# Order of the first transfers, casts and subtractions at the start of the first and of the merging run of a two-block kernel

## What is computed

```python
h = rms_norm(x, norm_w)
proj = h @ w_in
a_u, a_v, a_z, b_q, b_k, b_v, b_z, m_q, m_z, g = jnp.split(proj, split_at, axis=-1)
u = jax.nn.gelu(a_u, approximate=False)
vv = layer_norm(jax.nn.gelu(a_v, approximate=False), a_v_norm_w, a_v_norm_b)
y_a = chunked_spatial_gating(u, vv, a_spatial_w, a_spatial_b) * jax.nn.silu(a_z)
...
gates = jax.nn.sigmoid(g.reshape(bn, s, N_BRANCHES, D_MODEL) + gate_b)
merged = (gates[:, :, 0] * (y_a @ proj_a)
          + gates[:, :, 1] * (y_b @ proj_b)
          + gates[:, :, 2] * (y_m @ proj_m))
x = x + merged @ w_out
```

## Time and profile before

| | |
|---|---|
| median of 3 runs | 1872.83 us (1871.79 to 1872.91) |
| the profiled execution | 1871.02 us, its span 1869.2 us |
| TensorE busy | 1769.4 us |
| VectorE busy | 915.2 us |
| ScalarE busy | 654.0 us |
| GpSimd busy | 246.5 us |
| bytes moved | 123.07 MB, 66 GB/s over the span |

### The profile page before, as it was taken

How to read it: one execution, slowest core, us unless ns; L and a number is a source line. 1 busy time by engine, 2 the same in 40 slices (tenths; PEclk the granted TensorE clock), 3 DMA queues, 4 the chain that set the end, 5 groups by cost and what they waited for, 6 DMA issues and landing times. The chain is left out here.

```text
span 1869.2 us, 22280 instructions
## 1 busy us (share of the span) xinstructions
PE 1769.4 (95%) x8828; PEld 1435.2 (77%) x8828; DVE 915.2 (49%) x1504; ACT 654.0 (35%) x1204; POOL 246.5 (13%) x412
## 2 busy tenths in 40 slices
PE   6999989899999899799999999899999999999698
PEld 5788867688887788578888788688887777777587
DVE  5118887545334654383223322367142445657654
ACT  5224337512233333472212211233213353434531
POOL 3001210288601100000000000481000000000000
PEclk9999999899999999899999999899999999999799
DMA  4121100236322210111111121242623111000042
GB/s 137 51 68 46 46 22 3 87 104 185 109 80 88 75 34 23 59 43 43 51 51 54 40 58 30 79 150 79 140 50 93 34 35 35 23 23 35 23 147 102
DMA packets 146577, 123.07 MB, mean 66 GB/s; under 512 B 8859, under 2 KB 132106, under 8 KB 145802
## 3 DMA queue, kind: packets, MB, share of 16 engines
q1 hardware_dynamic: 146474, 121.65, 21.5%
HBM read 108.37 MB, written 13.26 MB: 65 GB/s over the span
## 5 line engine op out<-in xcount | busy, mean ns | idle before, releaser
L81 PE MATMUL psum<-hT,w_parts 128*128 128x512 f32 x3360 | 802.6, 396 | 20.1 <-DVE w_parts L182 13.4
L81 PEld LDWEIGHTS psum<-hT,w_parts 128*128 128x128 f32 x3360 | 634.5, 190 | 159.5 <-DVE w_parts L182 15.6
L182 DVE TENSOR_TENSOR w_parts<-w_raw,w_parts 128x1024 fp32r<-128x1024 f32 x104 | 133.1, 1280 | 491.4 <-ACT w_parts L178 491.2
L81 PE MATMUL psum<-h2T,w_parts 128*128 128x512 f32 x1248 | 300.6, 397 | 1.6 <-PEq L2144 1.1
L81 PEld LDWEIGHTS psum<-h2T,w_parts 128*128 128x128 f32 x1248 | 233.4, 190 | 51.3 <-issue 2.9
L81 PE MATMUL psum<-y_high,wp_parts 128*128 128x512 f32 x384 | 129.7, 398 | 9.6 <-DVE wp_parts L1421 9.3
L1373 ACT ACTIVATE gate<-psum,cols 128x512 f32<-128x512 f32 x48 | 33.1, 689 | 297.9 <-PE psum L81 297.9
L178 ACT CAST w_parts<-w_raw 128x1024 fp32r<-128x1024 f32 x104 | 108.3, 1041 | 74.6 <-DMA w_raw<-w_in 58.1
L81 PE MATMUL psum<-w_parts,y_parts 128*128 128x512 f32 x384 | 89.0, 394 | 7.7 <-DVE y_parts L1708 7.7
L81 PEld LDWEIGHTS psum<-y_high,wp_parts 128*128 128x128 f32 x384 | 72.5, 189 | 28.2 <-DVE wp_parts L1421 9.7
L81 PEld LDWEIGHTS psum<-w_parts,y_parts 128*128 128x128 f32 x384 | 73.2, 191 | 23.5 <-issue 8.1
(11 more groups left out here) (358 smaller groups left out, 2235.6 us busy)
## 6 DMA issues: line engine op xcount, KB each, us to landing
w_raw<-w_in SPq DMA_DIRECT2D x94, 512.0 KB, 3.9
middle_a<-ada_w SPq DMA_DIRECT2D x32, 384.0 KB, 3.6
w_raw<-w_out SPq DMA_DIRECT2D x16, 512.0 KB, 4.0
qkT<-x SPq DMA_DIRECT2D x8, 512.0 KB, 8.4
w_raw<-m_w_kv SPq DMA_DIRECT2D x8, 512.0 KB, 3.8
base<-x SPq DMA_DIRECT2D x8, 512.0 KB, 4.4
x_kept<-x_ring SPq DMA_DIRECT2D x8, 512.0 KB, 2.6
base<-x_kept SPq DMA_DIRECT2D x8, 512.0 KB, 3.6
```

Of the source, the lines that this page charges most:

```text
L81: last = pe.matmul(out, lhs(a, k), rhs(b, k), start=(k == 0 and n == 0), stop=(k == depth - 1 and n == 2))
L182: dve.tensor_tensor(self.parts[:, u, LO, :, :], self.raw[:, :, :], self.parts[:, u, HI, :, :].bitcast(F32), ALU.subtract).then_inc(self.lo ...
```

## The change

The first run: rows 2 and 3 of x are loaded ahead of the weights' first tile; ScalarE makes the roots of all four rows ahead of any cast; VectorE scales rows 2 and 3 ahead of moving rows 1 to 3 and of the weights' subtraction; TensorE turns four rows ahead of slot 0, and rows 4 and 5 within it. The merging run: the first tile of proj_b is the first load on the queue, the gate's second tile the second, and the three spatial loads come behind it (a new hook, `sync_second`); the two rows of y_b and the tile of proj_b are cast and subtracted ahead of everything else in `scalar_start` and `vector_start`.

```diff
@@ Dense.sync
                 w.load_tile(sp, self.tiles[n].view)
-            if n == 0:
-                for work in self.beside:
+            for work in self.beside:
+                if n == 0:
                     work.sync(sp, -1)
+                elif n == 1:
+                    work.sync_second(sp)
@@ FirstNorm
-        sp.dma_start(self.x[:, 1, :], self.src[1]).then_inc(self.x_loaded[1], 16)
+        for t in range(1, 4):
+            sp.dma_start(self.x[:, t, :], self.src[t]).then_inc(self.x_loaded[t], 16)
 
     def sync(self, sp, s):
         if s == -1:
-            for t in range(2, TT):
+            for t in range(4, TT):
                 sp.dma_start(self.x[:, t, :], self.src[t]).then_inc(self.x_loaded[t], 16)
...
         self.root(act, 2)
+        self.root(act, 3)
         self.split(act, 0)
+        self.split(act, 1)
         self.w.split_high(act, 0, 0)
-        self.root(act, 3)
-        self.split(act, 1)
-        self.root(act, 4)
         self.split(act, 2)
         self.split(act, 3)
+        self.root(act, 4)
         self.root(act, 5)
         self.w.split_high(act, 0, 1)
...
-        for t in range(TT):
-            self.scale(dve, t)
-            if t == 1:
-                dve.wait_ge(self.const_loaded, 32)
-            if t >= 1:
-                self.move(dve, t - 1)
-            if t == 2:
-                self.w.split_low(dve, 0, 0)
-            if t == 4:
-                self.split_low(dve, 3)
-            if t == 6:
-                self.w.split_low(dve, 0, 1)
+        self.scale(dve, 0)
+        self.scale(dve, 1)
+        dve.wait_ge(self.const_loaded, 32)
+        self.move(dve, 0)
+        self.scale(dve, 2)
+        self.scale(dve, 3)
+        for t in range(1, 4):
+            self.move(dve, t)
+        self.w.split_low(dve, 0, 0)
+        self.split_low(dve, 3)
+        self.scale(dve, 4)
+        self.scale(dve, 5)
+        self.move(dve, 4)
+        self.scale(dve, 6)
+        self.w.split_low(dve, 0, 1)
+        self.move(dve, 5)
+        self.scale(dve, 7)
+        self.move(dve, 6)
         self.move(dve, TT - 1)
...
-        for t in range(5):
+        for t in range(4):
             self.turn(pe, t)
...
-        if s in (0, 1):
-            self.turn(pe, 5 + 2 * s)
+        for t in {0: (4, 5), 1: (7,)}.get(s, ()):
+            self.turn(pe, t)
@@ Projections
+    def sync_start(self, sp):
+        self.load(sp, 0)
+
     def sync(self, sp, s):
-        if s == -1:
-            self.load(sp, 0)
-        elif s == 0:
+        if s == 0:
             self.load(sp, 1)
...
+    def scalar_start(self, act):
+        for r in self.splits(-1):
+            self.y_split_high(act, r)
+        self.wp_split_high(act, 0)
+
+    def vector_start(self, dve):
+        for r in self.splits(-1):
+            self.y_split_low(dve, r)
+        self.wp_split_low(dve, 0)
...
             self.y_split_high(act, r)
-        if s == 0:
-            self.wp_split_high(act, 0)
...
             self.y_split_low(dve, r)
-        if s == 0:
-            self.wp_split_low(dve, 0)
@@ SpatialValues
-    def sync(self, sp, s):
-        if s == -1:
-            sp.dma_start(self.wide, self.rows).then_inc(self.loaded, 16)
-            sp.dma_start(self.wT, self.spatial_dram).then_inc(self.loaded, 16)
-            sp.dma_start(self.bias, self.bias_dram).then_inc(self.loaded, 16)
+    def sync_second(self, sp):
+        sp.dma_start(self.wide, self.rows).then_inc(self.loaded, 16)
+        sp.dma_start(self.wT, self.spatial_dram).then_inc(self.loaded, 16)
+        sp.dma_start(self.bias, self.bias_dram).then_inc(self.loaded, 16)
@@ merge_run
-    split_at = {(1, 0): 0, (1, 1): 0, (2, 0): 12, (2, 1): 13, (2, 2): 14, (2, 3): 15, (0, 0): 28, (0, 1): 29}
+    split_at = {(1, 0): -1, (1, 1): -1, (2, 0): 12, (2, 1): 13, (2, 2): 14, (2, 3): 15, (0, 0): 28, (0, 1): 29}
```

More of the change, by code:

```diff
@@ L96, in sync_start @@
     def sync_start(self, sp):
+        pass
+    def sync_second(self, sp):
         pass
@@ L1432, in y_split_low @@
                           ALU.subtract).then_inc(self.y_low, 1)
+    def sync_start(self, sp):
+        self.load(sp, 0)
     def sync(self, sp, s):
-        if s == -1:
-            self.load(sp, 0)
-        elif s == 0:
+        if s == 0:
             self.load(sp, 1)
-        elif s % 2 and s // 2 + 2 < len(self.tiles):
+        elif s > 0 and s % 2 and s // 2 + 2 < len(self.tiles):
             self.load(sp, s // 2 + 2)
```

## The result

| | before | after |
|---|---|---|
| median, measured together | 1872.87 us (4 runs, 1871.79 to 1875.78) | 1858.74 us (4 runs, 1856.40 to 1859.85) |
| ratio | | 0.9916 [0.9901, 0.9931] |
| the profiled execution, its span | 1871.02, 1869.2 us | 1859.85, 1858.1 us |
| the same two kernels compared once more | 1873.30 us (11 runs) | 1859.65 us (6 runs), ratio 0.9929 [0.9914, 0.9943] |

The medians differ by 14.1 us in the first comparison and by 13.7 in the second; the ratios put it at 15.7 and 13.3. Between the two profiled executions the spans differ by 11.1.

What follows compares the result with a forecast made beforehand. TensorE, busy 1769.4 of 1869.2 us, was taken as the bound, with gains only where it waits or runs below full clock. -11.9 (merging run) - 0.8 (start) = -12.7, from 1872.83 to 1860.1 us; range 1857.2 to 1864.2.

Steps and rivals of the forecast that it cites:

- The forecast case: Whole kernel: merging run gains 11.9 us and the start 0.8, median 1860.1 us; chance 0.52.
- the start's term: First run: tile 0's second half starts at 41.1 instead of 41.88, 0.8 us gained of the first product's 2.5.
- The merging run's 11.9 us: Merging run: wait removed, 9.5 us, plus the clock no longer low behind it, 2.4 us.
- The wait removed, 9.5 us: Merging run, slot 0: TensorE no longer waits for the split of proj_b's first tile; 779.01 - 769.5 = 9.5 us.
- The clock behind it, 2.4 us: Merging run: with no pause the next 30 products take 6.87 us instead of 9.24, 2.4 us gained.
- rival 2: Merging run, slot 2: gate tile lands late, proj_b's second tile comes 2.2 us after TensorE; 1862.3 us, chance 0.10.
- The first product, 2.5 us earlier: Start: three operations of GpSimd and VectorE that exclude each other set the first product at 22.6 instead of 25.14.
- rival 1: Start: GpSimd served first at 34.6, row 7's scaling late, the start loses 1.5 us; 1862.4 us, chance 0.25.
- The start's two terms given back, 0.8 and 0.8: Start: row 4's transposes move into slot 0, +0.8 us; the longer standstill lowers the clock, 2.5 us lost against 1.7, +0.8.
- GpSimd's second group: Start: GpSimd works on row 4 from 32.2, ends row 6 about 39.9, holding row 7's subtraction until then, ending 41.0.
- Rival 3: Between the runs: the clock doesn't fall in the pause, 1.7 us more gained; 1858.4 us, chance 0.08.
- Rivals 4 and 5: Merging run's splits still late, 1872.0 us, chance 0.03; start slower through GpSimd winning five contested grants, 1875.4 us, chance 0.02.

Runs made afterwards that it cites:

- e2: Only the start's part of the change, the merging run as before, against the kernel before: 1871.18 us, ratio 1.0004 [0.9993, 1.0015].
- e8: The changed kernel with the gate's second tile loaded behind the three spatial loads: 1861.20 us, ratio to the kernel before 0.9931 [0.9916, 0.9946].
- e5: The changed kernel with row 2's low part on VectorE instead of GpSimd: 1859.25 us, ratio to the kernel before 0.9932 [0.9916, 0.9947].
- e1: Only the merging run's part of the change, the first run as before, against the kernel before: 1858.95 us, ratio 0.9937 [0.9923, 0.9950].
- the repeat: The changed kernel once more, unaltered, against the kernel before: 1859.65 us, ratio 0.9929 [0.9914, 0.9943].
- e3: The kernel before with only the merging run's new order of loads, casts and subtractions at their old places: 1868.18 us, ratio 0.9984 [0.9972, 0.9996].
- e11: The changed kernel with useless transposes in TensorE's pauses at the start and before the merging run: 1855.71 us, ratio to the kernel before 0.9898 [0.9883, 0.9913].
- e7: The changed kernel with 12 useless transposes at the end of the run before the merging run: 1859.29 us, ratio to the kernel before 0.9926 [0.9912, 0.9939].
- e10: The changed kernel with both of TensorE's pauses filled by useless transposes and row 2's low part on VectorE: 1854.03 us, ratio to the kernel before 0.9888.
- batch 1: The first group of follow-up runs on one chip, with the kernel before run beside them: 1871.89 us (21 runs, 1865.27 to 1876.12).
- e6: The changed kernel with 28 useless transposes while TensorE waits ahead of its first product: 1855.25 us, ratio to the kernel before 0.9911 [0.9894, 0.9927].
- e9: The changed kernel with the first run's loads in the old order, engines in the new: 1860.80 us, ratio to the kernel before 0.9926 [0.9913, 0.9940].

## Why the prediction was right in its mechanism, and where its size was wrong

The forecast case came in its mechanism, and more was gained than said: 14.1 us by the medians and 15.7 by the ratio, against 12.7. The median of 1858.74 us lies in the range, 1.4 us below the number. But by the ratio the time on the prediction's scale is 0.9916 x 1872.83 = 1857.1 us (1854.3 to 1859.9): 3.0 below the number and 0.1 below the range's lower end of 1857.2. The second comparison gives 1859.5 (1856.7 to 1862.1), inside the range. The gain of 12.7 us would be a ratio of 0.9932, just outside the first comparison's interval and inside the second's.

**The step that failed is the start's term, 0.8 us gained where the profile of after shows 2.2;** within it, above all, the 0.8 us given back to the clock, which was 0 there. The merging run's 11.9 us held (11.8). The second step is the range, which put the shifting of low clock in the untouched stretches at nothing. The bullets on the start, on what it is worth and on the span take these up.

- **The wait removed, 9.5 us.** Right. The projection of slot 0 moved by 9.42 us against the run's start. Its links held within 1 us: proj_b's cast at 764.06, the tile's subtraction ending at 765.5 (said: 766.4).
- **The clock behind it, 2.4 us.** Right: 30 products 6.88 us instead of 9.24. e2 shows the other side, where the wait came back and the 30 products behind it took 9.50 us again (781.41 to 790.91).
- **The gate tile and rival 2.** The tile landed early enough and the rival did not come about. Its condition and its place were right (e8: a wait of 2.43 us in slot 2, 2.2 said), but its price was too low by more than half. It counted the wait and not the clock that falls behind it; both together are 5.8 us in e8's profile.
- **The first product, 2.5 us earlier.** Right: 2.88 in the profile, 2.8 as mean. The three excluding operations are there one behind another, and e5, which moves one of them from GpSimd to VectorE, brings the product 1.2 us forward, as their sum gives. The Trainium skill, "SBUF — State Buffer", section "Who interferes with whom", says that a VectorE instruction with two SBUF inputs contends with a GpSimd instruction that reads SBUF; the trace agrees (1.76 and 3.36 us beside GpSimd, 1.22 without it).
- **Row 7's scaling, rival 1.** It rested on who is served first, and had 0.25. VectorE was: 1.58 us. In all five executions with the new order the second half starts between 39.5 and 41.9; none has the 43.4 of the rival.
- **The start's two terms given back, 0.8 and 0.8: the step that was mis-sized.** Row 4's transposes cost what was said (1.66 us for two rows against 0.83 for one). The clock term assumed 2.5 us lost in the new order against 1.7 in the old. It took the 2.5 from the restart at 779, where the low clock lasted for 5 us of work behind the stop. In after it lasted for less: it fell early in the pause, was 0.50 over 22 to 25.5 and back at 1.00 by 26.64, and the 12 products took 4.38 us as before: the term was 0. Over all executions it is 0.6, but of a quantity that itself runs from 0 to 2.4 us lost. The tail from row 7's transposes to the half tile was 4.92 us, where 5.2 was said (35.9 to 41.1) and 5.03 was before. So the start gained 2.2 us in the profile and 1.5 as mean, not 0.8; of the 1.4 us in the profile 0.4 are the first product's, 0.8 the clock's and 0.3 the tail's.
- **GpSimd's second group** is part of the same step. The prediction had it begin row 4 at 32.2, end row 6 at 39.9 and so hold row 7's subtraction until 41.0. It began at 30.09 and ended at 38.45, and the subtraction ended at 39.53. Of the 2.1 us at its beginning 0.3 are the earlier first product and 0.8 the clock. From its transposes to its low part row 4 took 3.45 us (26.64 to 30.09), as row 5 took 3.50 before (29.52 to 33.02), and that leaves 0.9 us for which the prediction gives no working. TensorE's stop ahead of the half tile was 1.13 us, where 2 was said.
- **What the start is worth in the end** stays open. The median of e2 puts it between 1.3 us gained and 2.8 lost. The ratios of e1 and of the change (0.9937 against 0.9916 and 0.9929) would give it 1.5 to 4, with intervals that overlap in part. With the mean of 1.5 from the profiles the sum is 11.8 + 1.5 = 13.3, the second comparison's gain; that doesn't show that it reaches the median.
- **Rival 3,** the clock not falling between the runs, had 0.10. Of the eleven profiled executions in which nothing fills that pause, one has it (e2, 5.7 us for 24 products); in seven they take 7.3 us and in three 8.2 or 8.3 (the repeat, e1, e3). The same pause, both ways: that fits what the Trainium skill says in "TensorE: Matmul & The Clock Gate", Part 1, that the gate's phase is free-running. No run here shows what decides between the two.
- **Rivals 4 and 5** did not come: the rows are cast at 761.70, at the run's first moment, and in the two contested grants that the rows let one read (near 17.8 and 33.2) VectorE was served.
- **The passage from the span to the median.** The sum is a difference on one execution, yet the two untouched stretches moved by +1.5 and +1.3 us between the two profiled executions. Over all fourteen, the first of them runs from 718.6 (e11) to 725.2 us (the repeat) with the same instructions, but for the 12 transposes of e7, e10 and e11. The granted clock over 45 to 755 us is 0.98 in e11 and 0.97 in the repeat, so stretches of low clock are at least part of what shifts. With a spread of 11 us between the runs of the kernel before in batch 1, four runs on each side don't fix a median to 1 us. The difference between 12.7 said, 14.1 and 13.7 measured, and 11.1 in the spans is of that size; no run here assigns it, and so it stays open what made the first comparison's ratio larger than the second's. A range that took the spread in would have reached lower than 1857.2.

## What to carry to other kernels

Look for the engine program's order ahead of an operation before its duration: a 0.4 us cast stood behind a transfer and a Gelu that its reader did not need, and moving it to the head of ScalarE's and VectorE's programs was worth 10.7 of the 11.8 us in the profile; moving the load alone was worth 4.7 (by the ratios 8.2 and 3.0). Price a stop of TensorE as wait plus low clock behind it, on both sides of the balance: here 2.4 us on top of 9.4, and 3.2 on top of 2.6 in e8. Where work ahead of a first product is shortened and the pause stays, see whether the clock gives the gain back (e5), and whether a few useless transposes in the pause hold it up (e6, e10).

## What the runs showed of the hardware

- **The clock shown at the start isn't the one granted.** In after the view gives 1.00 over the first 10 us, but the 8 transposes at 7.64 take 1.94 us, and 1.03 at 34.76. In e9 the view gives 1.00 from 0 to 45, its stretch 26:29 above too; yet the 12 products from 23.67 take 5.26 us to the next start (28.93), where 12 products take 2.84 in after (28.30 to 31.14). Its 8 transposes ahead of them, at 15.77, took 1.94 us as well: there the clock seems not to have risen at all before the first product. For the start of a kernel, read durations.
- **Order where VectorE and GpSimd exclude each other.** At the end of a GpSimd subtraction, VectorE, which had been waiting, was served ahead of GpSimd's next one: near 17.8 us (the weights' subtraction, asking since 17.11) and near 33.2 (row 7's scaling, asking since 32.17). The two moments are worked out from the ends of 18.87 and 33.75, less the 1.09 and 0.55 us that such an operation took behind GpSimd's end before. In both VectorE had asked first: the casts that GpSimd's next rows needed ended near 17.25 and 33.14. At 18.87 it is the other way round: GpSimd had asked since 17.78, VectorE's row 3 since 18.80, and the 3.36 us of that subtraction fit only if GpSimd was served. All three fit "who asked first".
- **A short pause can cost more than itself.** Behind 2.70 us between the runs, 24 products took 7.2 to 8.1 us from start to start instead of 5.6, in ten of eleven executions. TensorE had done little ahead of it either: 4 small transposes (0.63 us) behind another 0.87 us of idling. With that pause cut to 1.38 us by transposes, the clock stayed up in all three executions that have them (e7, e10, e11).
- **The clock's stretches move by themselves.** The same instructions ran with different stretches of low clock in each execution, and the spread from run to run goes with it: of the 21 runs of the kernel before in batch 1, the seven with the lowest granted clock (0.970 to 0.972) have a median of 1873.05 us, the seven with the highest (0.974 to 0.976) 1869.92.
